# Per-bank signals at the end of a layer's output, scaling on ScalarE, high parts first, and products beside the norm

## What is computed

```python
def rms_norm(x, g):
    y = x * lax.rsqrt(jnp.mean(x * x, axis=-1, keepdims=True) + RMS_EPS)
    return y * g

def swiglu(x, w_in, w_out):
    gate, up = jnp.split(x @ w_in, 2, axis=-1)
    return (jax.nn.silu(gate) * up) @ w_out

h = h + 0.5 * rms_norm(swiglu(rms_norm(h, g[0]), w_in[l, 0], w_out[l, 0]), g[1])
u = rms_norm(h, g[2])
m = rwkv7_time_mix(u, ...) if layer == 0 else swa_sinks(u, k_sh, v_sh, ...)
h = h + rms_norm(m, g[3])
h = h + 0.5 * rms_norm(swiglu(rms_norm(h, g[4]), w_in[l, 1], w_out[l, 1]), g[5])
# after layer 0:  kv = rms_norm(h, kv_norm_g) @ w_kv + b_kv
```

## Time and profile before

| What | us |
|---|---|
| Median of three runs | 2901.87 |
| The three runs | 2908.24, 2895.41, 2901.87 |
| The profiled execution | 2910.47 |
| Its span, first to last instruction | 2908.6 |
| TensorE busy in it | 2712.4 (93%) |
| GpSimd busy | 1769.0 (61%) |
| VectorE busy | 1079.9 (37%) |
| ScalarE busy | 611.2 (21%) |

### The profile page before, as it was taken

One profiled execution on the slowest core, in us unless ns is written; L12 is line 12 of the kernel. 1 busy time (PEld: TensorE's weight loads), 2 busy tenths in 40 slices (PEclk: granted clock), 3 DMA queues, 4 the chain that ended last, 5 costly groups with the idle time before them and its releaser, 6 DMA issues.

```text
span 2908.6 us, 49000 instructions
## 1 busy us (share of the span) xinstructions
PE 2712.4 (93%) x18506; PEld 2201.5 (76%) x18506; DVE 1079.9 (37%) x1618; ACT 611.2 (21%) x1159; POOL 1769.0 (61%) x1827
## 2 busy tenths in 40 slices
PE   8999988988887899999899998889999989999998
PEld 6888867667775688888788887667888877777677
DVE  2222044774455443320633312565333123122344
ACT  2111023523342111100211101342111011254111
POOL 5777658663221567777577775665677745645565
PEclk9999979989998999999899999998999989999998
DMA  4333313220000223333233332332333322322212
GB/s 130 94 94 94 94 44 83 75 60 4 4 3 9 64 85 94 97 95 98 62 95 95 96 95 76 124 116 81 91 94 98 95 73 82 91 62 66 78 41 80
DMA packets 116795, 226.00 MB, mean 78 GB/s; under 512 B 13088, under 2 KB 13856, under 8 KB 115616
## 3 DMA queue, kind: packets, MB, share of 16 engines
q1 hardware_dynamic: 114624, 209.46, 25.5%
q10 hardware_dynamic: 2016, 14.22, 1.4%
HBM read 221.53 MB, written 2.10 MB: 77 GB/s over the span
## 4 chain that ended last, share of the span: by engine, by line
PE 84%; DVE 6%; issue 3%; POOL 3%; ACT 2%; DMA 1%; SPq 0%; DVEq 0%; POOLq 0%; ACTq 0%
PE bank L221 22%; PE bank L223 22%; PE bank L222 22%; PE bank L299 2%; POOL turn_a L1838 1%; PE bank L1141 1%; PE bank L332 1%; DVE acc L295 1%; PE bank L1156 1%; PE bank L1095 1%; PE bank L2090 1%; POOL w_lo L207 1%; POOL w_raw L1337 1%; PE bank L2272 1%; PE bank L2081 1%
## 5 line engine op out<-in xcount | busy, mean ns | idle before, releaser
L207 POOL TENSOR_TENSOR w_lo<-w_raw,w_hi 128x512 fp32r<-128x512 f32 x778 | 1043.6, 1341 | 819.1 <-PE bank L223 744.3
L221 PE MATMUL bank<-x_hi,w_hi 128*128 128x512 f32 x2064 | 824.6, 399 | 27.8 <-POOL w_lo L207 13.0
L223 PE MATMUL bank<-x_hi,w_lo 128*128 128x512 f32 x2064 | 818.4, 397 | 0.0
L222 PE MATMUL bank<-x_lo,w_hi 128*128 128x512 f32 x2064 | 817.7, 396 | 0.0
L212 POOL TENSOR_SCALAR w_hi<-w_raw 128x512 fp32r<-128x512 f32 x778 | 558.4, 718 | 4.9 <-DMA w_raw<-weights 4.9
L221 PEld LDWEIGHTS bank<-x_hi,w_hi 128*128 128x128 f32 x2064 | 393.7, 191 | 121.1 <-issue 12.9
L223 PEld LDWEIGHTS bank<-x_hi,w_lo 128*128 128x128 f32 x2064 | 393.2, 191 | 88.3
L222 PEld LDWEIGHTS bank<-x_lo,w_hi 128*128 128x128 f32 x2064 | 393.4, 191 | 86.5 <-issue 0.2
L520 DVE TENSOR_TENSOR f<-bank,rstd 128x512 f32<-128x512 f32 x88 | 56.7, 686 | 632.4 <-PE bank L223 625.6
L221 PE MATMUL bank<-mid_hi,w_hi 128*128 128x512 f32 x704 | 276.6, 393 | 0.7 <-POOL w_lo L207 0.7
L223 PE MATMUL bank<-mid_hi,w_lo 128*128 128x512 f32 x704 | 276.6, 393 | 0.0
(11 more groups left out here) (401 smaller groups left out, 3269.3 us busy)
## 6 DMA issues: line engine op xcount, KB each, us to landing
w_raw<-weights SPq DMA_DIRECT2D x778, 256.0 KB, 2.6
ada_w<-ada_in ACTq DMA_DIRECT2D x8, 1536.0 KB, 6.7
h<-xT SPq DMA_DIRECT2D x4, 512.0 KB, 6.9
out<-f SPq DMA_DIRECT2D x8, 256.0 KB, 2.2
mask_b<-mask_b_in ACTq DMA_DIRECT2D x1, 640.0 KB, 4.8
spread<-spread_in SPq DMA_DIRECT2D x1, 512.0 KB, 7.3
window<-window_in ACTq DMA_DIRECT2D x1, 512.0 KB, 3.7
masks<-masks_in SPq DMA_DIRECT2D x1, 320.0 KB, 7.1
```

What stands on the lines that cost most here:

```text
L207: pool.tensor_tensor(w_lo[:, (n - 1) % RW, :], w_raw[:, (n - 1) % RS, :], w_hi[:, (n - 1) % RW, :].bitcast(F32), ALU.subtract).then_inc(w_ ...
L221: pe.matmul(o, w_hi[:, s, c], hi, start=first, stop=False)
L222: pe.matmul(o, w_hi[:, s, c], lo, start=False, stop=False)
L223: done = pe.matmul(o, w_lo[:, s, c], hi, start=False, stop=last)
```

## The change

Five edits, all at the seams between layers.

1. **Signals per bank.** In the second half of an output the last unit's products tell out_ready after each of the first three banks. ScalarE squares a bank on its own signal, and only the fourth waits for w_used.
2. **ScalarE scales the late tiles.** The four tiles of the second half are written to f by ScalarE (Copy, or Identity with a bias, with a gain per partition), three of them ahead of norm_root and the fourth behind. VectorE works the gains out in advance (out_gain, out_bias; 8 columns each).
3. **High parts first.** In block 0 of f0, f1, f3 and swa a unit's 8 matmuls that need only x_hi come first, and the 4 with x_lo last (early_products); kv_tensor likewise.
4. **Products beside the norm.** norm_beside puts products of the first two units of the block behind the pre-norm between the norm's steps: banks 2 and 3 of the first unit after norm_sums, those of the second after norm_wide, and banks 0 and 1 of both after the wait for rstd. This is block 1 of f0, f1, f3 and swa, and block 0 of f2.
5. **ada products.** 11 ahead of the post-norm's sums, 3 between sums and norm_wide, 10 behind.

The core of the diff:

```diff
+        def early_products(pe, outs, k, x0, n):
+            pe.wait_ge(w_lo_ready, n + 1)
+            pe.wait_ge(x_hi_ready, x0 + k + 1)
             s = n % RW
             for m, o in enumerate(outs):
                 c = slice(m * P, (m + 1) * P)
+                pe.matmul(o, w_hi[:, s, c], x_hi[:, k, :], start=k == 0, stop=False)
+                pe.matmul(o, w_lo[:, s, c], x_hi[:, k, :], start=False, stop=False)
+            pe.wait_ge(x_lo_ready, x0 + k + 1)
+            for m, o in enumerate(outs):
+                done = pe.matmul(o, w_hi[:, s, m * P:(m + 1) * P], x_lo[:, k, :], start=False, stop=k == KT - 1)
             done.then_inc(w_used, 1)
...
+        def norm_beside(pe, s, outs, n, last):
+            norm_sums(pe, s.pre, bank[s.pre_at][0])
+            if s.after is not None:
+                pe.wait_ge(s.after, 1)
+            def tiles(k, ms):
+                pe.wait_ge(x_lo_ready, s.x0 + k + 1)
+                return tile_products(pe, outs, ms, x_hi[:, k, :], x_lo[:, k, :], k == 0, k == last, n + k)
+            tiles(0, (2, 3))
+            norm_wide(pe, s.pre, bank[s.pre_at][1])
+            tiles(1, (2, 3))
+            pe.wait_ge(rstd_ready, s.rs + 1)
+            for k in range(2):
+                tiles(k, (0, 1)).then_inc(w_used, 1)
...
         def output_scalar(act, s):
             for half, set_ in enumerate((s.post_at, 1 - s.post_at)):
-                act.wait_ge(w_used, s.u1 + (half + 1) * s.rows)
+                if half == 0:
+                    act.wait_ge(w_used, s.u1 + s.rows)
                 for m in range(4):
                     k = 4 * half + m
+                    if half and m < 3:
+                        act.wait_ge(out_ready, 3 * (s.h0 // KT) + m + 1)
+                    elif half:
+                        act.wait_ge(w_used, s.u1 + 2 * s.rows)
                     square(act, s.post, k, bank[set_][m][:], ...)
-            norm_root(act, s.post, bank[s.post_at][0], D)
+            act.wait_ge(gain_ready, s.h0 // KT + 1)
+            for m in range(4):
+                k, o = 4 + m, bank[1 - s.post_at][m][:]
+                if m == 3:
+                    norm_root(act, s.post, bank[s.post_at][0], D)
+                if s.bias is None:
+                    act.activation(f[:, k, :], o, ACT.Copy, scale=out_gain[:, k:k + 1]).then_inc(f_late, 1)
+                else:
+                    act.activation(f[:, k, :], o, ACT.Identity, scale=out_gain[:, k:k + 1], bias=out_bias[:, k:k + 1]).then_inc(f_late, 1)
...
             for m in range(4):
-                scaled(0, m)
+                scaled(m)
                 add_square(dve, s.post, m)
-            dve.wait_ge(w_used, s.u1 + 2 * s.rows)
             for m in range(4):
                 add_square(dve, s.post, 4 + m)
-            for m in range(2):
-                scaled(1, m)
             norm_inverse(dve, s.post)
-            for m in range(2, 4):
-                scaled(1, m)
```

More of the change, by code:

```diff
@@ L1564, in kv_tensor @@
-                for t in range(TT):
-                    o, c = sb_[2 + t // 2][:, t % 2 * KV:(t % 2 + 1) * KV], slice(t * P, (t + 1) * P)
-                    pe.matmul(o, x_hi[:, k, c], hi[:, KV:], start=first and t % 2 == 0, stop=False)
-                    pe.matmul(o, x_lo[:, k, c], hi[:, KV:], start=False, stop=False)
-                    done = pe.matmul(o, x_hi[:, k, c], lo[:, KV:], start=False, stop=last and t % 2 == 1)
+                pe.wait_ge(w_lo_ready, n + 1)
+                pe.wait_ge(x_hi_ready, s.x0 - KT + k + 1)
@@ L1710, in swa_tensor @@
                         pe.wait_ge(x_lo_ready, s.x0 + KT + k + 1)
[L1711 removed]
+                    unit_products(pe, [o[:] for o in bank[set_]], x_hi[:, k, :], x_lo[:, k, :], k == 0, k == KT - 1, s.u1 + b * KT + k,
+                                  tell=out_ready if b and k == KT - 1 else None)
             def ada_products(first, last):
```

118 lines of the change are left out of this document (70 added, 48 removed).

## The result

The changed kernel takes **2867.74 us** (median of 4 runs, 2866.90 to 2868.98); the kernel before, run beside it on the same chip, 2903.30 us (2895.41 to 2908.24). The ratio is 0.9878, with a 95% interval from 0.9858 to 0.9898: 35 us faster, within about 30 to 41. The forecast was 2873 us, 28.5 us faster.

The account below looks back on a forecast made before the run. TensorE was taken to bound the kernel, with time to win only in its stops and low-clock stretches. Terms 11.0 + 2.7 + 1.7 + 8.4 + 4.7 = 28.5 us, off 2901.87, gave 2873 us; range 2858 to 2888.

Parts of the forecast that it names:

- What bounds the kernel: Whole kernel: TensorE is busy 2712.4 of 2908.6 us, so time is only where it stands still or runs slower.
- Outputs of f0, mix, f1, f2, f3: 2.2 us each: Edits 1 and 2: root 4.4 us behind the last product instead of 6.61; five outputs give 11.0 us (10.0 to 15.5).
- at that price they end at T0 + 2.5: At those outputs: VectorE's four adds, at 0.97 us each, end 2.5 us after the last product's end.
- What VectorE no longer does lay beside TensorE's sums and costs nothing: At those outputs: the scaling taken off VectorE had run during TensorE's sums, at no cost in time.
- swa's output: 2.7 us: Behind swa's output, with edit 5: f3's first product comes at 2000.8 instead of 2003.46, 2.7 us earlier.
- Edit 3: 1.7 us, two places: Block 0 starts with x_hi, 0.84 us earlier; counts in swa and f1 only, 1.7 us together (0 to 4.2).
- Edit 4, waits: 8.4 us, and the clock: 4.7 us: Pre-norms: products cover waits in five layers, 8.4 us; 2.4 GHz kept behind f0, f1 and f3, 4.7 us.
- Tail of the table load: Rival, chance 0.07: a tail behind the load delays the root 1.5 us at five outputs; 7.5 lost, 2881 us.
- Added waits: Rival, chance 0.07: some 60 new TensorE waits cost 0.2 to 0.39 us each; 2885 to 2897 us.
- The clock stays low: Rival, chance 0.03: norm_beside's pieces keep blocks from returning to 2.4 GHz, 16 us a block; three blocks give 2926 us.
- The base: Starting time for the forecast: the three runs' median, 2901.87 us, with the profiled execution at 2910.47, 8.6 above.
- What would show it: Signs: norm_sums waits under half of 26.3 us, root 4.2 to 4.6 behind last product; wrong if root waits for table.

Follow-up runs that it names:

- e7: Changed kernel, with GpSimd waiting for each output's last add before splitting the second and third unit behind it; 2862.98 us, ratio 0.9867.
- e5: Kernel before with edit 1 alone: banks are signalled, VectorE scales all late tiles; 2880.69 us in one run.
- e6: Kernel before with edit 2 alone: ScalarE scales late tiles but waits for the whole last unit; 2894.47 us in one run.
- e11: Changed kernel without edit 2; 2862.54 us, ratio 0.9860.
- e2: Kernel before with edit 3 alone, early_products and the keys' block in their new order; 2894.79 us, ratio 0.9971.
- e9: e8 with ScalarE's wait for the gains moved ahead of the squares, nothing else; 2856.39 us, ratio 0.9836.
- e8: e7 with ScalarE's root ahead of all four late scalings and the update waiting for each late tile; 2864.69 us, ratio 0.9871.

## Why the prediction was right, and where it was not

The forecast of 2873 us had 2867.74 inside its range, and the sum of 28.5 us stands against 33.5 us (second trace of before) or 36.6 (first trace, of which 6.5 is f0's slow pace) in the touched stretches. The mechanisms were the right ones, the sizes met in part by luck: the outputs' terms missed in both directions and cancelled, and edit 4 gave more than was forecast. None of the rivals came true. Point by point:

- **What bounds the kernel.** Right: the gain came from the seams, and TensorE's matmuls elsewhere kept their pace.
- **Outputs of f0, mix, f1, f2, f3: 2.2 us each.** The mechanism is right, the chain of the sum was mis-sized in two places. The root came at T0 + 4.15, 5.02, 4.80, 5.03 and 5.08 and not at 4.4. The step that failed is "at that price they end at T0 + 2.5": 0.97 for an add was the mean of four in the earlier trace rows, of which the first two stood beside GpSimd's splitting (1.26 and 0.91) and the last two did not (0.69 each). Started 2.1 us earlier, the last three of the four all ran into GpSimd's splitting (0.92, 1.57, 0.91); the four took 4.4 us, and 3.08 when e7 took GpSimd away. The table load, forecast for T0 + 4.2, was ready at T0 + 4.0 behind f1, f2 and f3 and was not last there. At f0 more was gained than forecast, 4.1 us: GpSimd mostly folds small pieces there, the adds took 0.69 each, the sums start at T0 + 1.98, and the table load, ready at T0 + 4.14, is what the root waits for. With edit 3, whose gain lies in the same seams, 12.7 us were forecast; the five seams gave 4.1, 2.3, 2.5, 2.3 and 1.6 against the second trace of before, 12.7 again (12.3 against the first). The right total comes from a miss at four seams and a surplus at f0.
- **What carries it.** The prediction told edits 1 and 2 as one term. e5, e6 and e11 split it: edit 1 is all of it. "What VectorE no longer does lay beside TensorE's sums and costs nothing" was the right step; its other half, that moving it therefore gains nothing, wasn't drawn.
- **swa's output: 2.7 us.** From swa's last product to f3's pre-norm it is 38.0 us instead of 40.7 and 41.0, and f3's first product comes 2.7 us earlier. Right, with two small misses that cancel: the root came at T0 + 4.74 and not at 4.4, with the table load's end, and the first product 3.9 us behind the spread's end and not 4.3.
- **Edit 3: 1.7 us, two places.** e2 shows 0.65 to 0.69 us in three places, 2.0 us. Where it was sized at nothing (the keys' block in front of f2), the block started 0.69 us earlier and the first product behind the norm came 0.5 us earlier. It does wait for VectorE's rewrites and reciprocal, as forecast, but these came 0.5 us earlier too; that they would not was the step without a reason.
- **Edit 4, waits: 8.4 us, and the clock: 4.7 us.** e3, which has edit 4 alone, gave 18.8 us against the second trace (3.3 in f0, 4.4 in f1, 5.0 in f2, 4.4 in swa, 1.7 in f3) for 13.1 forecast. The mechanism is right: products fill the waits, and all five windows stand at 1.00. Three sizes were off. The 1.25 us of swa, f1 and f3 measured 1.6 to 1.7 where the clock had been high before (swa against the first trace, f3 against the second). The spread was priced at its full 1.16 us, but the next product starts 0.81 us behind the spread's start (1803.23 and 1804.04). In f2 the term of 2.5 was the middle of 2.1 to 3.0; the spread took 1.16 us, the end that gives 3.0, and the 1.3 of the clock that I had not counted came on top: 4.3 of the 4.8 to 5.0 measured. And I took one trace's clock for the kernel's: swa's gap left the clock at 2.4 GHz in the first trace (158.2 us to the output), and at 1.2 in the second, which took 161.0; f3's did it the other way round. Before the change f1 took 346.5 and 347.8 us and f3 346.5 and 345.0; with edit 4 every trace has 343.3. So the 4.7 us fit the low windows of the first trace, and another execution has another sum.
- **Tail of the table load.** In the changed kernel itself the root behind f0 waits for the load alone and starts 0.01 us behind its end (387.48 and 387.49); in e7 the load ends at 1356.69 and the root starts at 1356.71, with nothing else to wait for. Ahead of the load there is none either: the scalings end at 1355.40 and it starts at 1355.41. There is no tail here. The Trainium skill (ScalarE: Activation LUTs, What ACT_TABLE_LOAD costs) adds 1.38 us of drain to the 1.28; this trace agrees with the 1.28 and contradicts the drain.
- **Added waits.** The products in norm_beside start at 1802.07, 1802.30, 1802.54 and 1802.77, 0.23 us apart. The waits cost nothing that shows.
- **The clock stays low.** It did not.
- **The base.** I set the sum against the median, and not against the slow first trace. That was the step that kept the forecast near: the first trace held 6 to 7 us of f0's slower pace, which no edit could have taken.

Of the marks named in "What would show it", two failed though the forecast held. norm_sums waits 15.7 us, not less than 13, and the root came 4.2 to 4.6 us behind the last product at none of the five outputs: a little earlier behind f0, later behind the other four. Behind those four, both are the miss of the adds. And one mark of being wrong appeared without its cause: behind f0 and swa the root did wait for the table, which the three scalings held up, and no tail followed.

## What to carry to other kernels

Start a reduction's tail on the first finished piece of the last unit: one signal per bank was worth all of the 14 to 17 us of the outputs, and moving work off an engine that was idle anyway was worth nothing. When a chain is moved to an earlier time, price each of its steps beside what the other engines do at that time, and not by its old mean. Two traces of the kernel before show which stretches are the kernel's and which the execution's, and that is worth having before a gain or a loss of less than 10 us is explained.

## What the runs showed of the hardware

- VectorE's 128x512 add with two operands in SBUF took 0.69 us alone. At the outputs of mix, f1, f2 and f3 an add that began while GpSimd's pass L214 ran took 0.91 or 0.92 us, one that began 0.25 us behind L209's start 1.56 to 1.62. L214 took 1.05 to 1.11 us there and 0.62 in e7, away from the adds; L209 took 1.26 to 1.29. Beside the small folds at f0 the adds took 0.69.
- At a granted clock of 1.00 TensorE's 512-column matmuls came every 0.2333 us through one execution's f0 and every 0.2289 in all others. The granted clock doesn't show it.
- A gap at a pre-norm of the same program left the clock at 2.4 GHz in one execution and at 1.2 in the next (swa's window 1.00 and 0.52, f3's 0.54 and 1.00). The four sums of an output, starting 3.15 us behind the last product, took 1.02 us in some traces (granted clock 1.00) and 1.84 in others (0.50); at 1.83 us behind it, 1.15 to 1.16 behind f1 in e7 to e9 (0.83 in e9). The spread behind f1 took 2.08 us in the changed kernel and 2.08 in e9, where it started at T0 + 3.5.
- In e8, where the root had two waits to serve, the table load waited for the sums; behind f1 it began at T0 + 3.06 instead of 0.80 (e9), and the root came 1.3 us later. The timeline shows such a wait as a releaser on the ACT_TABLE_LOAD row.
